# A two-block transformer kernel on one core: what TensorE computes over two waits ahead of the second feed forward

## The chip, the cores and the metric

The kernel is one program on one core of a Trainium2 chip. TensorE (PE in the profile) multiplies, with its weight loads shown apart as PEld. VectorE is DVE, ScalarE is ACT, GpSimd is POOL, and SyncE (SP) issues the transfers. The metric is the device time of one execution in microseconds. The kernel before took 2340.14 us, the median of three runs (2338.34, 2341.20 and 2340.14 us).

## The reference, cut to what matters

Two transformer blocks follow each other over 256 tokens of width 2048. The first mixes by a forgetting attention and a short convolution and has a SwiGLU feed forward. The second mixes by three branches and has a feed forward with a convolution. The place of the change lies between the second block's output projection and its feed forward:

```python
x = x + gt1 * (jnp.concatenate([o_mla, o_na, o_fn], axis=-1) @ w_out[l])
...
h2 = rmsnorm_2(x, g_ffn[l]) * (1 + sc2) + sh2
x = x + gt2 * conv_ffn(h2, w_up[l], conv_w[l], conv_b[l], w_down[l])
```

The root mean square norm of `x` takes a sum over all 2048 features of each token, and no part of `h2` is there before that sum.

## The kernel before, in words

All activations lie transposed in SBUF: features on the 128 partitions, the 256 tokens along the row, 16 tiles of 128 features. The weights are streamed from HBM once. Each chunk of 128x1024 values comes into one of four slots (`raw`), ACT rounds it to `hi` (line 586), DVE subtracts to get `lo` (line 1746), and TensorE makes three products for each tile of 128x128 weights (lines 1178 to 1180): `hi` by the rounded input, `hi` by the input's rest, `lo` by the rounded input. `hi`, `lo` and the inputs `hs`, `ysa`, `ysb` are of the type float32r, which TensorE takes in one pass. A product of operands of the type float32 ("plain" here) is made in two passes, so it leaves two records of matmul and two of weight load in the trace.

The order of the work is written out by hand, engine by engine. Engines meet in semaphores, and each engine runs its own list strictly in order. Around the change TensorE's list is:

1. the last products of the output projection `out2` (lines 1178 to 1180 on `ysa` and `ysb`);
2. `residual_stats("out2", "ffn2")`: plain products of one column (line 1247) that sum the squares of `x` over the partitions, two on `ssum` and four on `sqb`. ACT then takes the root (`std`, line 610), and DVE the reciprocal (line 1807);
3. a first `bridge`, whose products have no reader (line 1706);
4. `spread("ffn2", 5)`: it waits for the reciprocal and spreads it over the partitions with two plain products of 128 columns (line 1228);
5. a second `bridge`;
6. the first products of the feed forward, on `hs`. Before the three products of each of the first four feature tiles, TensorE waits for that tile: DVE multiplies `hg` by the spread row (line 2562), ACT rounds to the first half of `hs` (line 1118), and DVE makes the second half (line 2567).

The bridge's products go to bank 6 of PSUM, which nothing reads at that time. `ysb` is the rounded input of the projection that has just ended; its place is written next by the hidden layer of the feed forward, and `hg` and `hs` lie behind it.

Of the kernel before, what the change touches and what calls it, by code (L numbers as in the profile page):

```python
# [31 lines left out]
P = 128  # L32
D = 2048
KT = D // P
NX = 256
# [127 lines left out]
def build(nc, tokens, ctx_tokens, cols_d, tables1_d, tables2_d, stream, mod_stream, c_rows, na_bias_d, w_fnet_d, out):  # L163
    stack = ExitStack()
    with stack:
# [6 lines left out]
        start = -(-top[0] // 64) * 64  # L172
        top[0] = start

        def at(name, shape, dt, offset):
            size = 4 * int(np.prod(shape[1:]))
            assert offset + size <= limit, (name, offset + size, limit)
            return nc.alloc_sbuf_tensor_at(name, shape, dt, offset=offset)

        def keep(name, shape, dt=F32):  # L180
            offset = top[0]
            top[0] += -(-4 * int(np.prod(shape[1:])) // 64) * 64
            return at(name, shape, dt, offset), offset
# [9 lines left out]
        tabs, _ = keep("tabs", [P, N_TABS])  # L193
# [14 lines left out]
        ssum = at("ssum", [P, 2, NX], F32, o_rstd)  # L208
        mix_r = at("mix_r", [P, N1], F32, o_rstd)
        _, o_work = keep("work_slab", [P, 2, 4, N1])  # L210
        sq = at("sq", [P, 2, 4 * N1], F32, o_work)
        xn = at("xn", [P, 2, 4 * N1], F32, o_work)
# [45 lines left out]
        ysb = at("ysb", [P, 8, 2, NX], F32R, o)  # L258
# [26 lines left out]
        ps = stack.enter_context(nc.psum_tensor("ps", [P, 8, 512], F32))  # L285
# [7 lines left out]
        def tab(name):  # L293
            return tabs[:, TABS[name][0]:TABS[name][0] + TABS[name][1]]

        ident, mean = tab("ident"), tab("mean")
# [214 lines left out]
        def _(sp_):  # L511
# [29 lines left out]
            for ly in LAYERS:  # L541
                def body(it, ly=ly):
                    for hf in range(ly.halves):
                        for j in range(ly.c):
                            a = ahead(ly, it, hf, j)
                            if a is not None:
                                load(a[0], a[1])
                            for m, (where, _, _) in enumerate(ly.dots):
                                if where == hf * ly.c + j:
                                    load_mod(ly.mbase + m + it * len(ly.dots), m % 2)  # L550
                            if ly.name == "kv1" and (hf, j) == (0, 2):
                                sp_.dma_start(cols[:, KT:N_COLS], cols_d[:, KT:N_COLS]).then_inc(tables_in, 16)
                                sp_.dma_start(tabs[:, 0:N_TABS1], tables1_d).then_inc(tables_in, 16)
                            if ly.name == "kv1" and (hf, j) == (1, 2):
                                sp_.dma_start(cbx[:, :, :].rearrange("p a n -> p (a n)"), c_rows[0].partition_broadcast(P))\
                                   .then_inc(c_in, 16)
                            if ly.name == "up1a" and (hf, j) == (1, 0):
                                sp_.dma_start(cx[:, bass.ds(2 * it, 2), :], ctx_tokens[:, bass.ds(2 * it, 2), :]).then_inc(ctx_in, 16)
                            if ly.name == "dn1a" and (hf, j) == (0, 0):
                                sp_.dma_start(cx[:, bass.ds(it + 12, 1), :], ctx_tokens[:, bass.ds(it + 12, 1), :]).then_inc(ctx_in, 16)  # L560
                            if ly.name == "up1b" and (hf, j) == (0, 2):
                                sp_.dma_start(tabs[:, bass.ds(it * TAB_PIECE + TABS["swap"][0], TAB_PIECE)],
                                              tables2_d[:, bass.ds(it * TAB_PIECE, TAB_PIECE)]).then_inc(late_in, 16)
                            if ly.name == "conv1" and (hf, j) == (9, 0):
                                sp_.wait_ge(y_ready, HEADS)
                                sp_.dma_start(cbc[:, :, :].rearrange("p a n -> p (a n)"), c_rows[1].partition_broadcast(P))\
                                   .then_inc(c_in, 16)
# [582 lines left out]
        def _(pe):  # L1150
# [73 lines left out]
            def spread(name, bank, values=None):  # L1224

                pe.wait_ge(inv_ready, NTH[name] + 1)
                for th, rows in token_tiles(name):
                    ins = pe.matmul(ps[:, bank, th * P:th * P + rows], (tok_inv(name) if values is None else values)[0:rows, th:th + 1].to_broadcast([rows, P]),
                                    ident[0:rows, 0:rows], start=True, stop=True)
                ins.then_inc(rstd_ready, 1)  # L1230

            def residual_stats(name, norm, gain=False, before_last=None):
                halves = LY[name].its * LY[name].halves
                kinds = [(ssum, sqb, 0)] + ([(gsum, gsqb, 2)] if gain else [])
                tiles = 1 if name in FOLDED else 2
                last = tiles - 1 if name in ADDED else tiles + 1
                pe.wait_ge(sum_added, ADD0[name] + halves + 1 + (name in FOLDED) + 2 * (name in ADDED))
                pe.wait_ge(std_ready, NTH[norm])
                for i in range(last + 1):
                    if i >= tiles:  # L1240
                        pe.wait_ge(sum_sq, SUMS[name] + halves + i - tiles + 1)
                    if i == last and before_last is not None:
                        before_last()
                    for total, part, c0 in kinds:
                        x = total[:, i, :] if i < tiles else part[:, 1, i - tiles, :]
                        for th in range(2):
                            ins = pe.matmul(ps[:, 4 + c0 + th, 0:1], x[:, th * P:th * P + P], mean[:, 0:1],
                                            start=i == 0, stop=i == last)
                ins.then_inc(stat_ready, 1)
# [453 lines left out]

            def bridge(n):
                for _ in range(n):
                    pe.matmul(ps[:, 6, 0:NX], ident, tabs[:, 0:NX], start=True, stop=True)

            residual_stats("out2", "ffn2")
            bridge(2)
            spread("ffn2", 5)  # L1710
            bridge(4)
            for turn, (hf, j) in enumerate(KV_ORDER):
                if turn == 7:
                    opener(7, hs[:, 0])
# [28 lines left out]
        def _(dve):  # L1743
# [10 lines left out]
            def mod_dot(ly, it, m):  # L1754

                _, x_only, i = ly.dots[m]
                half = i % 2
                n = ly.mbase + m + it * len(ly.dots)
# [1011 lines left out]
```

## Time and profile before

| | us |
|---|---|
| median of three runs | 2340.14 |
| the profiled execution | 2339.23 |
| its span, first instruction to last | 2337.4 |
| PE busy in the span | 2327.6 |
| PEld busy | 2264.7 |
| DVE busy | 1662.2 |
| ACT busy | 1123.2 |

The profiled execution's own time is 1.8 us above its span, and 0.9 us below the median of the runs.

Three of the views need a word. In a timeline or a chain a row begins with its start and its duration in us, counted from the span's start; "x8" says that eight records in a row were merged, and the duration runs from the first one's start to the last one's end. Matmuls overlap, so the time from one start to the next is shorter than one record: for n merged records it is (duration minus one record) / (n - 1). In brackets stands the idle time ahead of a row, and what ended it. A row of "windows" gives the busy time and the count of each engine in a stretch, in the order PE, PEld, DVE, ACT, POOL, and then the granted share of TensorE's full clock (PEclk), the share of the DMA engines and GB/s. A row by line (L1725) gives the shortest, median and longest record in ns.

### The profile page before, as it was taken

The numbers are of one execution on the slowest core, as the hardware profiler recorded it, in microseconds if no ns is written. First come the engines' busy times: TensorE is split into PE (matmuls) and PEld (weight loads), VectorE is DVE, ScalarE is ACT, GpSimd is POOL, SyncE is SP. The second block draws the span as 40 slices with busy tenths as digits, with TensorE's granted clock in tenths as the row PEclk, the third lists the DMA queues.
The fourth block names the chain that finished last, engine by engine and source line by source line (L and its number), as shares of the span: only waits on it lengthen the run. The fifth ranks groups of instructions, "written<-read, shape, count | busy, mean of one in ns | idle before, by whom it ended". The sixth has DMA issues, their size and how long they took to land.

```text
span 2337.4 us, 49745 instructions
## 1 busy us (share of the span) xinstructions
PE 2327.6 (100%) x19268; PEld 2264.7 (97%) x19268; DVE 1662.2 (71%) x2504; ACT 1123.2 (48%) x1501; POOL 0.2 (0%) x4
## 2 busy tenths in 40 slices
PE   9999999999999999999999999999999999999998
PEld 9998899999999999999988989799999999999998
DVE  6676678788878887888887755467666566655665
ACT  6454446554445553445632342456554355544554
POOL 0000000000000000000000000000000000000000
PEclk9999999999999999999999999999999999999999
DMA  7875567588778887887567722054666656665664
GB/s 282 290 280 195 191 229 243 199 293 305 267 257 291 292 291 241 270 289 263 203 225 255 253 75 91 19 190 163 201 194 193 194 189 191 198 194 190 196 191 144
DMA packets 141889, 509.19 MB, mean 218 GB/s; under 512 B 15824, under 2 KB 17360, under 8 KB 141392
## 3 DMA queue, kind: packets, MB, share of 16 engines
q1 hardware_dynamic: 141776, 507.60, 64.9%
q8 instruction: 81, 1.33, 0.2%
q14 instruction: 32, 0.26, 0.0%
HBM read 505.44 MB, written 2.10 MB: 217 GB/s over the span
## 4 chain that ended last, share of the span: by engine, by line
PE 98%; DVE 1%; DMA 0%; ACT 0%; issue 0%; SPq 0%; ACTq 0%; DVEq 0%
PE ps L1178 30%; PE ps L1180 30%; PE ps L1179 30%; PE ps L1543 1%; PE ps L1561 1%; PE ps L1206 1%; PE ps L1207 1%; PE ps L1208 1%; PE ps L1364 1%; PE ps L1552 0%; PE ps L1346 0%; PE ps L1389 0%; PE ps L1370 0%; DMA raw<-in_stream 0%; PE ps L1609 0%; PE ps L1347 0%
## 5 line engine op out<-in xcount | busy, mean ns | idle before, releaser
L1746 DVE TENSOR_TENSOR lo<-raw,hi 128x1024 fp32r<-128x1024 f32 x751 | 915.7, 1222 | 477.5 <-ACT hi L586 473.9
L586 ACT ACTIVATE hi<-raw 128x1024 fp32r<-128x1024 f32 x753 | 797.1, 1061 | 950.6 <-PE ps L1180 843.5
L1178 PE MATMUL ps<-hs,hi 128*128 128x256 f32 (+1 forms) x3056 | 857.9, 281 | 0.4 <-DVE hs L2567 0.3
L1180 PE MATMUL ps<-hs,lo 128*128 128x256 f32 (+1 forms) x3056 | 857.2, 280 | 0.0
L1179 PE MATMUL ps<-hs,hi 128*128 128x256 f32 (+1 forms) x3056 | 857.2, 280 | 0.0
L1178 PEld LDWEIGHTS ps<-hs,hi 128*128 128x128 f32 x3056 | 573.6, 188 | 6.2 <-DVE hs L2567 0.8
L1179 PEld LDWEIGHTS ps<-hs,hi 128*128 128x128 f32 x3056 | 573.9, 188 | 5.2
L1180 PEld LDWEIGHTS ps<-hs,lo 128*128 128x128 f32 x3056 | 573.6, 188 | 5.1
L1178 PE MATMUL ps<-hid,hi 128*128 128x256 f32 x1408 | 388.6, 276 | 0.0
L1180 PE MATMUL ps<-hid,lo 128*128 128x256 f32 x1408 | 388.6, 276 | 0.0
L1179 PE MATMUL ps<-hid,hi 128*128 128x256 f32 x1408 | 388.6, 276 | 0.0
L1179 PEld LDWEIGHTS ps<-hid,hi 128*128 128x128 f32 x1408 | 264.3, 188 | 0.0
L1178 PEld LDWEIGHTS ps<-hid,hi 128*128 128x128 f32 x1408 | 264.3, 188 | 0.0
L1180 PEld LDWEIGHTS ps<-hid,lo 128*128 128x128 f32 x1408 | 264.3, 188 | 0.0
L1776 DVE SCALAR_TENSOR_TENSOR wm<-wm,cbx 128x1024 f32<-128x1024 f32 x192 | 233.7, 1219 | 4.9 <-DMA wm<-in_mod_stream 4.9
L1178 PE MATMUL ps<-xs,hi 128*128 128x258 f32 (+2 forms) x760 | 221.1, 291 | 0.4 <-DVE lo L1746 0.4
L1180 PE MATMUL ps<-xs,lo 128*128 128x258 f32 (+2 forms) x760 | 216.3, 285 | 0.0
L1179 PE MATMUL ps<-xs,hi 128*128 128x258 f32 (+2 forms) x760 | 215.8, 284 | 0.0
L1178 PEld LDWEIGHTS ps<-xs,hi 128*128 128x128 f32 x760 | 142.9, 188 | 4.6 <-issue 2.7
L1179 PEld LDWEIGHTS ps<-xs,hi 128*128 128x128 f32 x760 | 143.9, 189 | 0.0
L1180 PEld LDWEIGHTS ps<-xs,lo 128*128 128x128 f32 x760 | 142.9, 188 | 0.0
L600 ACT ACTIVATE cv<-ps,cols 128x256 f32<-128x256 f32 x88 | 44.9, 560 | 78.5 <-PE ps L1180 78.5
(335 smaller groups left out, 2537.8 us busy)
## 6 DMA issues: line engine op xcount, KB each, us to landing
raw<-in_stream SPq DMA_DIRECT2D x753, 512.0 KB, 4.3
wm<-in_mod_stream SPq DMA_DIRECT2D x192, 512.0 KB, 4.9
out_tokens<-y_final SPq DMA_DIRECT2D x4, 512.0 KB, 3.7
h<-in_tokens SPq DMA_DIRECT2D x3, 544.0 KB, 9.2
cx<-in_ctx_tokens SPq DMA_DIRECT2D x6, 256.0 KB, 5.9
cbx<-in_c_rows SPq DMA_DIRECT2D x1, 1024.0 KB, 7.5
cbc<-in_c_rows SPq DMA_DIRECT2D x1, 1024.0 KB, 7.9
na<-in_na_bias SPq DMA_DIRECT2D x1, 1024.0 KB, 4.7
```

Of the source, the lines that this page charges most:

```text
L586: act.activation(hi[:, slot, :], raw[:, slot, :], ACT.Copy).then_inc(hi_done, 1)
L600: act.activation(cv[:, t, hf, :], ps[:, 2 * hf + t, 0:NX], ACT.Identity, bias=dcol("conv2_b", it * 2 + c), scale=dcol("conv2_w1", it * 2 + ...
L1178: pe.matmul(acc_, hi[:, slot, w], x_hi, start=kt == 0, stop=False)
L1179: pe.matmul(acc_, hi[:, slot, w], x_lo, start=False, stop=False)
L1180: ins = pe.matmul(acc_, lo[:, slot, w], x_hi, start=False, stop=kt == last_k)
L1206: pe.matmul(acc_, x_hi, hi[:, slot, w], start=first, stop=False)
L1207: pe.matmul(acc_, x_lo, hi[:, slot, w], start=False, stop=False)
L1208: ins = pe.matmul(acc_, x_hi, lo[:, slot, w], start=False, stop=last)
L1364: ins = pe.matmul(ps[:, 7, NX:2 * NX], vtok[0:rows, kt, hd * P:hd * P + P], pt1[0:rows, kt, :], start=kt == 0, stop=kt == 2)
L1543: ins = pe.matmul(ps[:, score_bank2(hd, qt, local), :], q, k, start=i == 0, stop=i == len(terms) - 1)
L1746: dve.tensor_tensor(lo[:, slot, :], raw[:, slot, :], hi[:, slot, :].bitcast(F32), ALU.subtract)\
L1776: dve.scalar_tensor_tensor(w, w, 1.0, cbx[:, half, :], ALU.mult, ALU.mult, accum_out=mine[:, half:half + 1]).then_inc(wm_used, 1)
```

## The change

The products of `bridge` become another kind. Before, each was a plain one: the identity as weights, 256 columns of the table `tabs` as moving operand. Now each takes 128 columns of `ysb` as weights and 128 columns of another tile of `ysb` as moving operand, both float32r. Two become 14 ahead of the spread row, and four become 26 behind it. They go to the same bank, take no wait and signal nothing, as before.

```diff
             def bridge(n):
                 for _ in range(n):
-                    pe.matmul(ps[:, 6, 0:NX], ident, tabs[:, 0:NX], start=True, stop=True)
+                    pe.matmul(ps[:, 6, 0:P], ysb[:, 1, 0, 0:P], ysb[:, 2, 0, 0:P], start=True, stop=True)
 
             residual_stats("out2", "ffn2")
-            bridge(2)
+            bridge(14)
             spread("ffn2", 5)
-            bridge(4)
+            bridge(26)
```

On TensorE, from the last product of the output projection to the first of the feed forward, the list before is this; `ps` is PSUM, `std` the reciprocal row, a product is written output, inputs and shape, and xN counts products, not passes:

```order
 L1180 MATMUL ps<-ysa,lo 128x256
 L1247 MATMUL ps<-tabs,ssum 128x1 x2
 L1247 MATMUL ps<-tabs,sqb 128x1 x4
 L1706 MATMUL ps<-tabs 128x256 x2
 L1228 MATMUL ps<-tabs,std 128x128 x2
 L1706 MATMUL ps<-tabs 128x256 x4
 L1178 MATMUL ps<-hs,hi 128x256
```

The same stretch of TensorE's list in the changed kernel:

```order
 L1180 MATMUL ps<-ysa,lo 128x256
 L1247 MATMUL ps<-tabs,ssum 128x1 x2
 L1247 MATMUL ps<-tabs,sqb 128x1 x4
 L1706 MATMUL ps<-ysb 128x128 x14
 L1228 MATMUL ps<-tabs,std 128x128 x2
 L1706 MATMUL ps<-ysb 128x128 x26
 L1178 MATMUL ps<-hs,hi 128x256
```

Only the two groups of line 1706 differ; nothing moved past anything, and the lists of the other engines and of the transfers are the same.

## Rows read from the trace of the kernel before

**Rows 1.** The page: its first line, and the shares of the chain that ended last.
```profile
span 2337.4 us, 49745 instructions
PE 98%; DVE 1%; DMA 0%; ACT 0%; issue 0%; SPq 0%; ACTq 0%; DVEq 0%
```

**Rows 2.** The chain that ended last, 1603.9 to 1608.6 us, in order of time.
```profile
1603.90 0.97 PE ps L1706 x4
1604.88 0.46 PE ps L1228 x4
1605.36 0.43 DVE hg L2562
...
1608.61 0.39 PE ps L1178
```

**Rows 3.** Timeline of TensorE's matmuls (PE), 1603.8 to 1609.1 us.
```profile
1603.77 1.11 PE L1706 MATMUL ps<-tabs 128*128 128x256 f32 x4
1604.71 0.61 PE L1228 MATMUL ps<-tabs,std 128*128 128x128 f32 x4
1605.16 1.89 PE L1706 MATMUL ps<-tabs 128*128 128x256 f32 x8
1607.05 0.36 PE L1178 MATMUL ps<-hs,hi 128*128 128x256 f32 x1
...
1607.95 0.38 PE L1178 MATMUL ps<-hs,hi 128*128 128x256 f32 x1 [0.32 <-DVE hs L2567]
...
1609.07 0.33 PE L1178 MATMUL ps<-hs,hi 128*128 128x256 f32 x1
```

**Rows 4.** Timeline of TensorE's weight loads (PEld), 1602.8 to 1608.1 us.
```profile
1602.85 0.97 PEld L1247 LDWEIGHTS ps<-tabs,sqb 128*128 128x128 f32 x8 [0.32 <-ACT sqb L823]
1603.74 0.73 PEld L1706 LDWEIGHTS ps<-tabs 128*128 128x128 f32 x4
1604.50 0.63 PEld L1228 LDWEIGHTS ps<-tabs,std 128*128 128x128 f32 x4
1605.05 1.60 PEld L1706 LDWEIGHTS ps<-tabs 128*128 128x128 f32 x8
...
1607.95 0.19 PEld L1178 LDWEIGHTS ps<-hs,hi 128*128 128x128 f32 x1 [0.52 <-DVE hs L2567]
1608.06 0.19 PEld L1179 LDWEIGHTS ps<-hs,hi 128*128 128x128 f32 x1
```

**Rows 5.** Timeline of DVE: the reciprocal, and a tile of `hs`.
```profile
1604.23 0.17 DVE L1807 RECIPROCAL std<-std 128x2 f32<-128x2 f32 x1 [1.50 <-ACT std L610]
...
1607.41 0.48 DVE L2567 SCALAR_TENSOR_TENSOR hs<-hg,mod,hs 128x256 fp32r<-128x256 f32 x1
```

**Rows 6.** Weight loads by line: transposes of 16, of 128 columns, the bridge's.
```profile
L1357 PEld LDWEIGHTS ps<-tabs,p x16: 90/90/90, 167.2 to 283.6; 128*16 128x16 f32 x16
...
L1725 PEld LDWEIGHTS ps<-tabs,hg_final x32: 138/141/223, 2327.6 to 2331.4; 128*128 128x128 f32 x32
...
L1706 PEld LDWEIGHTS ps<-tabs x12: 190/190/192, 1603.7 to 1606.5; 128*128 128x128 f32 x12
```

**Rows 7.** The page: weight loads of float32r weights in the feed forwards.
```profile
L1178 PEld LDWEIGHTS ps<-hs,hi 128*128 128x128 f32 x3056 | 573.6, 188 | 6.2 <-DVE hs L2567 0.8
```

**Rows 8.** Windows: around the bridges, in the feed forward behind, and at the end.
```profile
1603.60:1607.00 3.40, 3.40 (x19) 2.79 (x18) 1.50 (x5) 2.46 (x5) 0.00 (x0) 1.00 0.20 81
1607.00:1610.40 3.40, 3.03 (x22) 2.62 (x22) 2.91 (x5) 1.18 (x3) 0.00 (x0) 1.00 0.00 0
...
1612.00:1640.00 28.00, 28.00 (x249) 27.95 (x248) 23.76 (x35) 18.96 (x28) 0.00 (x0) 1.00 0.53 174
...
2335.00:2337.40 2.40, 0.00 (x0) 0.00 (x0) 0.00 (x0) 0.00 (x0) 0.00 (x0) 0.62 0.65 242
```

**Rows 9.** Timeline of PE at the span's start.
```profile
1.50 5.49 PE L1275 MATMUL ps<-sq 128*128 128x256 f32 x12 [1.50 <-DVE sq L1847]
...
7.87 0.29 PE L1270 MATMUL ps<-xs,lo 128*128 128x272 f32 x1
```

**Rows 10.** Waits of PE, 1605 to 2320 us: in total, times, longest.
```profile
PE ps L1178 <- DVE hs L2567: 0.3, 1, 0.3
```

## Prediction

> **What bounds the kernel now.** I read the chain first: TensorE makes up 98% of it over 2337.4 us [rows 1], so a change on TensorE's list counts where it lies on that chain. Then the stretch of the change. The chain there runs through the first bridge, the spread row and DVE's `hg`, and comes back to TensorE at 1608.61, where it waits for a tile of `hs` [rows 2]. The second bridge is not in that list: it lies beside DVE's and ACT's work. So the first bridge can move the end, and the second only if it outlasts the tiles. Last, from 1605 us to 2320 the list of TensorE's waits has one entry, 0.3 us for `hs` [rows 10]. Behind this stretch nothing waits that could take up a delay: what is lost or won here stands in full at the end.
>
> **Is there a wait to be won?** The reciprocal ends at 1604.23 + 0.17 = 1604.40 [rows 5]. A tile of `hs` that DVE ends at 1607.41 + 0.48 = 1607.89 is followed by its weight load at 1607.95 [rows 4, 5], so waking takes 0.06, and the spread row's load could start at 1604.46. It starts at 1604.50, and its product, behind the bridge's last, at 1604.71 [rows 3, 4]. With nothing ahead, the product would start one load later than its load: 0.11, from 1607.95 to 1608.06 [rows 4]. That is 1604.57. The present bridge holds the chain up by 0.14 us, and this is the most that any other bridge can win.
>
> **The price of one new product.** No row of before shows a float32r product of 128 columns, so I bound it. Call the time from one to the next s.
> - By columns alone: in the feed forward 248 float32r products of 256 columns start in 28.00 us, 0.113 each [rows 8]. Half the columns give s = 0.057.
> - By weight loads: the eight one-column passes of line 1247 have next to nothing to stream, and still their loads stand (0.97 - 0.19) / 7 = 0.111 apart [rows 4]. The record of a float32r load lasts 188 ns and of a plain one 190 [rows 6, 7]; at 16 columns it is 90, so 128 columns cost 100 ns above a base that overlaps. A load of a transpose is 141, so other kinds exist, but float32r is not that kind. After a wait, with two loads free to run ahead, float32r loads too are 0.11 apart [rows 4]. This gives s = 0.111.
> - If under 256 columns the type were worked off as plain, in two passes with a load each: s = 2 x 0.111 = 0.222.
>
> I take 0.111, the nearest row in kind, since the weights of each product are loaded anew even though they are the same. 0.057 and 0.222 stay as the ends.
>
> The Trainium skill, TensorE: Matmul & The Clock Gate, section LDWEIGHTS, prices a load by its columns at 1.2 GHz, an estimate of 0.107 for 128, and the trace's 0.111 agrees. Its section Back-to-back issue gap instead gives some 81 ns per product for streams of load and product at 128 columns; by that 14 would cost 1.13 us and not 1.55. It speaks against my reading, and the one-column rows go against it here, so it stands as a rival.
>
> **The first bridge, 2 plain to 14.** Removed: two products, four passes of 256 columns, starting at 1603.77 [rows 3]. Added: 14 loads and products. The first load is at 1603.74 [rows 4]; the spread row's load follows 14 s later, at 1603.74 + 1.55 = 1605.29, and its product one load later, at 1605.40. Before it stood at 1604.71: later by 0.69. In general the delay is 14 s + 0.11 - 0.97, and at least -0.14. The waiting instruction behind it is the spread row itself, and behind that come `hg`, `hs` and all of the feed forward, which shift with it.
>
> **The second bridge, 4 plain to 26.** Before, it begins loading at 1605.05 and hides until the first tile's load, its product at 1607.05 [rows 3, 4]. That start has slack: the fourth tile's first product is at 1609.07 [rows 3], and ahead of it lie nine products, 9 x 0.113 = 1.02 us; if they start by 1608.05 in one piece, nothing is late. (The second tile is there by 1607.95, the third by 1608.61, both ahead of their turn then.) In the new kernel, on a clock shifted by the first bridge's delay, the 26 loads end at 1605.05 + 26 x 0.111 = 1607.94, and the first product starts at 1608.05. The cover is used up exactly and the cost is 0.0; at s = 0.113 it would be 0.05. If the cover were gone, each further ns of s costs 26 ns here and 14 in the first bridge.
>
> **The sum.** +0.69 + 0.0 to 0.05: about +0.7 us. Against the profiled execution: 2339.23 + 0.7 = 2339.9. The median of the runs was 0.91 above that execution, so 2340.9 us. DVE, ACT and the transfers have the same lists; they start 0.7 later in this stretch and wait as before. Bank 6 has no reader, and `ysb` is not rewritten until the hidden layer.
>
> **The clock.** PEclk is 1.00 in both windows of the stretch, the second of them with 0.37 us of idle time on PE [rows 8]. At its low level (1.2 GHz) the span begins: line 1275, two passes each, starts every (5.49 - 0.63) / 11 = 0.44 us, twice the 0.216 of line 1706 [rows 3, 9]. In the changed kernel the array streams 57 of each 111 ns in the bridges, where it now streams all the time, so less is streamed, though PE is never long without a product. The clock is lost in this trace only at the very end, PEclk 0.62 after the last product [rows 8]. I take it to hold.
>
> **Rivals.**
> 1. Columns alone decide, s = 0.057. Then the 14 are over at 1603.77 + 0.80 = 1604.57, just when the reciprocal lets the row go, so the full 0.14 is won; the 26 take 1.48 and end before `hs` is there. Time 2340.0. For it: two loads can overlap one product in the first of a burst. Against it: the one-column rows.
> 2. Loads overlap in part, s = 0.081: 1.13 + 0.11 - 0.97 = +0.27, the second bridge hidden, 2340.4. This is the page's figure above; the rows show no such spacing for full loads.
> 3. The slower side: the products are not one-pass ones on the chip, s = 0.222. First bridge: 3.11 + 0.11 - 0.97 = +2.25. Second: 5.77 from 1605.05 is 1610.82, its first product of the feed forward 1610.93 against 1608.05, +2.88. Together +5.1, 2345.3, slower by 0.22%. It decides from s = 0.211 on. For it: no float32r product under 256 columns is in the trace. Against it: on the changed list each is one entry, and those of 256 columns leave one record each [rows 3].
> 4. The clock falls in the stretch because half as much is streamed. At the start it took from 1.50 to about 7.6 us of products to rise (a record of 272 columns is back at 0.29 by 7.87) [rows 9]. 6.1 us at half speed cost 3.05, with the 0.7 makes +3.8, 2343.9. Should it fall in the first bridge and rise only after 6.1 us of dense work, the bridges run at twice 0.111 as in rival 3, and it is 5.1 + 3.05 = +8.2, 2348.3. Over 0.2% it comes if the low level lasts more than (4.7 - 0.7) x 2 = 8 us. The Trainium skill (same page, section Why this matters for your kernels) ties the loss to gaps without products; by that rule it would not fall here, and no row of before shows a stretch like the new one.
>
> **How the numbers follow.** Forecast (s of 0.108 to 0.125, +0.6 to +1.2) 0.65; rival 1 0.12; rival 2 0.07; rival 3 0.09; rival 4 0.05; something unseen 0.02. The runs of before lie 1.1 to 2.9 us apart, so medians of few runs move by about 1 us, more than most of these cases differ. About 0.2%, 4.7 us, is what a measurement of this kernel can tell from no change. Rivals 1 and 2 and the forecast lie inside; of rival 3 about half, with the runs' spread, lies above it, of rival 4 a third. Slower by over 0.2%: 0.07; faster: 0.01; within: 0.92. The range runs from 2338.8 (rival 1 less 1.2) to 2343.6 (the forecast's upper end, and rival 4's nearer case by the lower half of its spread).
>
> **What would show it.** In the profile after: 40 records on line 1706, one for each product, loads 0.111 apart, merged to about 1.6 and 3.0 us; the spread row's first product near 1605.4; DVE's first `hg` near 1606.05; no wait of PE for `hs` any more, or one under 0.1, and the fourth tile's first product near 1609.8; PEclk 1.00 throughout. Eighty records, or starts 0.06 or 0.08 apart, would make the price wrong; a spread row at 1604.6 is rival 1; a PEclk under 1.00 in this stretch is rival 4.

## The result, and the profile after

| | before | changed |
|---|---|---|
| median, us (13 runs each) | 2340.69 | 2345.47 |
| lowest to highest | 2338.34 to 2341.67 | 2340.27 to 2349.64 |
| ratio to before, 95% interval | | 1.0017 (1.0010 to 1.0024) |
| mean granted clock of a run | 1.000 in the profiled one | 1.000 in 5 runs, 0.996 to 0.998 in 8 |

The changed kernel is 4.8 us slower, and the spread of its runs tells more than the median: they fall into two groups. Five lie at 2340.3 to 2341.4 us, where the forecast of 2340.9 stood. Eight lie at 2343.9 to 2349.6 us, and these eight have the lower mean clock. The profile taken was one of the first group (2340.86 us, span 2338.6, clock 1.000), so at first it shows only the steps on the path, not the loss.

The changed kernel's matmuls, from the sums of squares to the tenth product on `hs` (start, duration, as in [rows 3]):

```profile
1603.37 1.05 PE L1247 MATMUL ps<-tabs,sqb 128*128 128x1 f32 x8 [0.24 <-ACT sqb L823]
1604.28 1.76 PE L1706 MATMUL ps<-ysb 128*128 128x128 f32 x14
1605.88 0.66 PE L1228 MATMUL ps<-tabs,std 128*128 128x128 f32 x4
1606.29 3.10 PE L1706 MATMUL ps<-ysb 128*128 128x128 f32 x26
1609.23 0.33 PE L1178 MATMUL ps<-hs,hi 128*128 128x256 f32 x1
...
1610.34 0.28 PE L1178 MATMUL ps<-hs,hi 128*128 128x256 f32 x1
```

Its weight loads in the two bridges, which answer to those of [rows 4]:

```profile
1604.26 1.64 PEld L1706 LDWEIGHTS ps<-ysb 128*128 128x128 f32 x14
...
1606.27 2.98 PEld L1706 LDWEIGHTS ps<-ysb 128*128 128x128 f32 x26
```

Forty records for forty products: they are one-pass ones. The loads start (2.98 - 0.19) / 25 = 0.112 us apart. Absolute times moved by 0.5 us ahead of the change already, so I count from the first product on `sqb`: 1603.37 here, 1602.85 before. The spread row's product comes 2.51 us behind it and came 1.86 behind it (+0.65). The first product on `hs` comes 5.86 behind it; the forecast's 1608.05, with 0.69 added, is 5.89. The tenth, the first of the fourth tile, comes 6.97 behind it and came 6.22 (+0.75): the nine products between take 1.11 us, not the forecast 1.02, and that is the last 0.1.

The chain of the changed kernel (compare [rows 2]):

```profile
1603.37 1.05 PE ps L1247 x8
1604.42 1.62 PE ps L1706 x14
1606.04 0.50 PE ps L1228 x4
1606.54 2.85 PE ps L1706 x26
1609.39 0.17 PE ps L1178
```

Where the chain ran through DVE and ACT, it now runs through the second bridge: the time in which that bridge was hidden behind their work is used up. A window over the stretch shows nothing amiss, and that is the trap:

```profile
1604.00:1608.00 4.00, 4.00 (x37) 4.00 (x37) 1.28 (x4) 2.58 (x6) 0.00 (x0) 1.00 0.20 79
```

PE is "busy" 4.00 of 4.00 us. But a record of a 128-column product lasts 275 ns, and its columns stream in about 57 (an estimate: half of the 0.113 us at which products of 256 columns start [rows 8]). With a product every 0.112 us the array streams about half of the time.

### The profile page after: what moved, and what is told of

The parts are those of the page before. It is cut to its first block, busy times and chain, and to the rows that moved or that the text cites. A ratio compares the mean times of both kernels' runs of the same rounds, so it can differ in the third digit from the quotient of the medians.

```text
span 2338.6 us, 49801 instructions
## 1 busy us (share of the span) xinstructions
PE 2328.6 (100%) x19296; PEld 2266.8 (97%) x19296; DVE 1662.0 (71%) x2504; ACT 1123.4 (48%) x1501; POOL 0.2 (0%) x4
## 4 chain that ended last, share of the span: by engine, by line
PE 98%; DVE 1%; DMA 0%; ACT 0%; issue 0%; SPq 0%; ACTq 0%; DVEq 0%
PE ps L1178 30%; PE ps L1180 30%; PE ps L1179 30%; PE ps L1543 1%; PE ps L1561 1%; PE ps L1206 1%; PE ps L1207 1%; PE ps L1208 1%; PE ps L1364 1%; PE ps L1552 0%; PE ps L1346 0%; PE ps L1389 0%; DMA raw<-in_stream 0%; PE ps L1370 0%; PE ps L1609 0%; PE ps L1347 0%
```

## The experiments

All were timed in 10 or 11 runs each, beside the kernel before on the same chip. Its median was 2340.05 us (33 runs) beside the changed kernel again, 256 columns, "7 and 15" and "none"; 2339.98 (33 runs) beside "first only", "second only" and the two plain ones; 2340.23 (20 runs) beside 192 and 64 columns. "Low clock" counts the runs with a mean granted clock of 0.998 or less. The path is read in each kernel's one profile as above, from the first product on `sqb` to the 10th and to the 100th on `hs`, against 6.22 and 16.49 us before (the changed kernel's first profile: +0.75 and +0.68). The last column is the stretch at the low level in that profile.

| kernel | median | ratio (95%) | low clock | 10th | 100th | low stretch |
|---|---|---|---|---|---|---|
| changed, again | 2345.70 | 1.0019 (1.0010 to 1.0028) | 8 of 11 | +5.41 | +5.52 | 10.2 us |
| 256 columns | 2342.14 | 1.0009 (1.0000 to 1.0018) | 0 of 11 | +1.06 | +1.39 | none |
| 192 columns | 2342.47 | 1.0006 (0.9997 to 1.0015) | 1 of 11 | +2.35 | +2.28 | 3.4 us |
| 64 columns | 2346.23 | 1.0023 (1.0014 to 1.0033) | 10 of 10 | +5.99 | +7.13 | 13.7 us |
| 7 and 15 | 2340.38 | 1.0003 (0.9994 to 1.0012) | 3 of 11 | -0.08 | -0.08 | none |
| none | 2341.42 | 1.0006 (0.9997 to 1.0015) | 9 of 11 | +0.19 | +1.57 | 6.8 us |
| first only | 2341.58 | 1.0007 (0.9998 to 1.0016) | 4 of 11 | +1.62 | +1.62 | 3.4 us |
| second only | 2339.47 | 0.9999 (0.9990 to 1.0008) | 1 of 11 | +0.05 | 0.00 | none |
| plain, 4 and 7 | 2341.14 | 1.0004 (0.9995 to 1.0013) | 0 of 11 | +1.01 | +0.94 | none |
| plain, 1 and 4 | 2339.66 | 0.9998 (0.9989 to 1.0007) | 0 of 11 | -0.15 | +0.23 | none |

Of the 86 runs of the kernel before that stand beside these, none is at 0.998 or less. The count has a limit: the profiles also show 0.3 to 3.7 us of the span's end at the low level, so a fall of 3.4 us shows as 0.998 or 0.999 and can be missed. "Low clock" counts the longer falls.

**The changed kernel again**, no edit.

> The changed kernel once more, 14 and 26 products of 128 columns. In 8 of its 13 runs the mean granted clock was 0.996 to 0.998 and the time 2343.9 to 2349.6 us; in the other 5 it was 1.000 and 2340.3 to 2341.4. Theory A (TensorE's array streams only half of the time in the stretch of the bridges, and its clock falls to the low level there in some executions): about half of the runs again at a mean clock under 0.999 and 3 to 8 us longer, and a profile of such a run shows PEclk under 1.00 from about the second bridge on, nowhere else. Theory B (the slow runs have a cause that is not in this stretch, such as transfers): the time is lost elsewhere, or spread over the span, and the share of slow runs does not follow the bridges.

(The change had 8, not 9, of its 13 runs at the low clock, where later expectations say 9 or 17 of 24: it is 16 of 24 with these.) Measured: 8 of 11 at the low clock, 2345.2 to 2347.2 us; the other three at 2340.1 to 2341.7. This time the profile is of an execution in which the clock fell. Its matmuls:

```profile
1603.28 1.05 PE L1247 MATMUL ps<-tabs,sqb 128*128 128x1 f32 x8 [0.24 <-ACT sqb L823]
1604.20 2.50 PE L1706 MATMUL ps<-ysb 128*128 128x128 f32 x14
1606.49 1.16 PE L1228 MATMUL ps<-tabs,std 128*128 128x128 f32 x4
1607.30 5.79 PE L1706 MATMUL ps<-ysb 128*128 128x128 f32 x26
1612.89 0.52 PE L1178 MATMUL ps<-hs,hi 128*128 128x256 f32 x1
1613.21 0.41 PE L1179 MATMUL ps<-hs,hi 128*128 128x256 f32 x1
```

and its windows (the column behind POOL is PEclk):

```profile
1602.00:1605.00 3.00, 2.68 (x23) 2.39 (x22) 1.34 (x5) 2.19 (x6) 0.00 (x0) 1.00 0.55 184
1605.00:1615.20 10.20, 10.20 (x50) 10.20 (x50) 6.45 (x13) 4.10 (x9) 0.00 (x0) 0.50 0.01 5
1615.30:1620.00 4.70, 4.70 (x44) 4.70 (x43) 1.65 (x2) 1.29 (x2) 0.00 (x0) 1.00 0.33 115
```

The clock falls to 0.50, that is 1.2 GHz, at 1605.0, in the middle of the first bridge, and comes back at 1615.3, some 2.4 us after the dense products on `hs` have begun. In between TensorE works at half the pace: the 26 products last 5.79 us and not 3.10, and those of 256 columns start 0.21 us apart and not 0.113. The tenth product on `hs` is 5.41 us late, the 100th 5.52. Apart from the span's two ends the clock is low nowhere else, so theory B falls for this run: the time is lost here.

**The same products with 256 columns.** Equal count and, by the loads, nearly equal time, but the array streams throughout.

```diff
-                    pe.matmul(ps[:, 6, 0:P], ysb[:, 1, 0, 0:P], ysb[:, 2, 0, 0:P], start=True, stop=True)
+                    pe.matmul(ps[:, 6, 0:NX], ysb[:, 1, 0, 0:P], ysb[:, 2, 0, 0:NX], start=True, stop=True)
```

> The same 14 and 26 one-pass products, but of 256 columns. By the weight loads (0.111 us) and the columns (0.113) they take nearly the same time, so the path is the same +0.7 to 0.8 us, but the array streams all of the time. Theory A: the clock is 1.000 in all runs, all within 2340 to 2343 us, median about 2341.5, ratio to before 1.0003. Theory B: slow runs as in the changed kernel, at a mean clock of 0.997 and 2344 to 2349 us. A third reading (it is the float32r products on ysb, or so many in a row, that lower the clock) also gives slow runs here.

Measured: no run at a low clock, as theory A has it. But the median is 2342.1 and not 2341.5, and the highest run 2344.4 and not 2343: in the profile the products of the second bridge started 0.12 us apart, not 0.113, and those of the feed forward behind them 0.118 (last section).

```profile
1605.50 3.36 PE L1706 MATMUL ps<-ysb 128*128 128x256 f32 x26
```

The two highest runs (2343.6 and 2344.4 us) are at 0.999; whether they hold a short fall is not shown. The reading that float32r products on `ysb` as such bring the long falls is out.

**192 columns** and **64 columns**, each with `ps[:, 6, 0:c]` and `ysb[:, 2, 0, 0:c]`, c = 192 or 64; the loads set the same pace.

> 14 and 26 one-pass products of 192 columns. The weight loads still set the pace (0.111 us; the columns would need 0.085), so the path is as in the changed kernel, +0.7 us, but the array streams three quarters of the time, not half. Theory A (the share of time in which the array streams decides, through the clock): the clock falls in clearly fewer runs than with 128 columns (17 of 24 so far), 0 to 3 of 11, median 2341 to 2342. Rival (any stream of float32r products bound by weight loads lowers the clock, whatever its columns): 7 or 8 of 11 at a mean clock of 0.996 to 0.998 and 2345 to 2347 us.

> 14 and 26 one-pass products of 64 columns, loads again 0.111 us apart: the path is +0.7 us or 0.05 less, and the array streams a quarter of the time. Theory A: the clock falls in nearly all runs (9 to 11 of 11) at a mean clock of 0.996 to 0.998, median 2345.5 to 2348. Rival: as with 128 columns, 7 or 8 of 11, median 2345.5.

Measured: 64 columns lose the clock in all 10 runs, 128 in 16 of 24, 192 clearly in one of 11 (its median of 2342.5 us is above the expected 2341 to 2342). But the profile of 192 shows a short fall in a run that counts as 0.999:

```profile
1605.60:1609.00 3.40, 3.40 (x18) 3.40 (x18) 2.08 (x5) 1.12 (x3) 0.00 (x0) 0.50 0.00 0
1609.00:1613.00 4.00, 4.00 (x37) 4.00 (x37) 3.24 (x7) 2.32 (x6) 0.00 (x0) 1.00 0.02 4
```

Five of its runs lie at 2339.2 to 2340.4 and six at 2342.5 to 2344.3 us, so falls of this length in about half of them are likely, though only the one is shown. With 64 columns the low level lasted longest, to 1618.0 us:

```profile
1602.00:1604.30 2.30, 1.98 (x17) 1.69 (x15) 1.12 (x3) 1.54 (x4) 0.00 (x0) 1.00 0.47 155
1604.40:1617.90 13.50, 13.50 (x65) 13.50 (x65) 8.36 (x15) 4.64 (x10) 0.00 (x0) 0.50 0.07 19
```

The number of products, of loads and their pace (0.112 us at the full clock, 0.213 at the low one) are one and the same with 64, 128 and 192 columns; only the columns differ, and with them how often the clock is low for long, and how long. The rival (any stream bound by loads) falls on 192 columns; between 64 and 128 the counts alone (10 of 10, 16 of 24) could still be chance.

One row of the kernel with 64 columns limits what may be said of the cause (line 1709 is the bridge's there):

```profile
1604.14 3.02 PE L1709 MATMUL ps<-ysb 128*128 128x64 f32 x14
```

The clock fell at 1604.32, 0.18 us behind the bridge's first product, when two of the 40 had started. In that execution the bridge can hardly have brought the fall; it can only have kept the clock low. What ran ahead of it, the sums' one-column products and the waits between them, stands in every kernel here, in the one before too.

**Shorter bridges of the new kind**: `bridge(7)` and `bridge(15)`.

> 7 and 15 products of 128 columns, so that both bridges last as long as before: 0.78 and 1.67 us against 0.86 and 1.72. On the path nothing is lost (0.0 to -0.1 us). Theory A: the array streams half of the time in as short a stretch as before; the clock falls in fewer runs than in the changed kernel, but in some; fast runs at 2340. If it is only the length of the bridges that matters (more time at half streaming), none is slow. Theory B: as many slow runs as in the changed kernel, or none, without relation.

Measured: the path is back (-0.08 us), and three of 11 runs, at 2341.5, 2344.0 and 2345.1 us and 0.997 or 0.998, still lose the clock. So half streaming loses it even in a stretch as short as before, but in fewer runs (3 of 11 against 16 of 24, which with so few runs makes it likely and not more). How long the stretch is seems to count as well.

**No bridge**: `bridge(0)` twice.

> No bridge products at all. The spread row's product starts when the reciprocal is there: 0.14 us won on the path, TensorE idle for some 0.6 us ahead of the spread row and 1.9 us ahead of the first tile of hs. Theory A: the array streams least of all, so the clock falls at least as often as in the changed kernel, and longer; fast runs 2340.0, slow ones 2344 or more. Theory B: no relation to streaming; time 2340.0 in all runs.

Measured: the clock is lower in nearly all runs, yet the median rises by 1.4 us only, and not one run is at the 2344 us or more that I expected of slow ones. The profile's windows:

```profile
1602.00:1606.00 4.00, 2.88 (x21) 2.32 (x19) 1.70 (x6) 2.77 (x6) 0.00 (x0) 1.00 0.45 158
1606.10:1612.80 6.70, 5.32 (x23) 5.14 (x24) 5.64 (x13) 3.52 (x8) 0.00 (x0) 0.50 0.00 0
```

Here the clock falls later (1606.1), lasts 6.8 us, and in part of it TensorE waits for `hs` anyway; the dense products begin 1.4 us into it and are not kept waiting by a bridge. I had reckoned with how often it falls and not with what stands in the low stretch. The experiment shows what the plain bridge is worth: 1.6 us at the 100th product in the one profile, 1.4 in the medians, where the interval of the ratio still includes none.

**One bridge of each kind**: 14 new products and 4 plain; then 2 plain and 26 new. Of the first kernel's edit one place is shown; the lines by which `bridge` chooses the kind are left out.

```diff
-            bridge(26)
+            bridge(4, plain=True)
```

> Only the first bridge changed: 14 products of 128 columns, then 4 plain ones. The path: the first bridge's +0.7 us and nothing in the second. Theory A (the clock falls because the array streams only about half of the time over the whole stretch from the sums to hs): the half streaming ends with the spread row, after some 3.5 us, then 1.7 us of full streaming follow; the clock falls in fewer runs than the 9 of 13 and 8 of 11 of the full change, 0 to 3 of 11, median 2340.8, slow ones 2345 to 2347. Rival (the first bridge alone brings the fall): as many slow runs as in the full change.

> Only the second bridge changed: 2 plain products, then 26 of 128 columns. The path: the 26 products just fill the time until the tiles of hs are there, +0.0 to 0.1 us. Theory A: 2.9 us of half streaming behind 0.9 us of full streaming; the clock falls in some runs, fewer than with both (2 to 6 of 11), median 2340.1, slow ones 2343 to 2346. Rival (the second bridge alone brings the fall): 7 or 8 of 11 at a mean clock of 0.997.

Measured for the first alone: 4 of 11 clearly low and not 0 to 3, 2341.6 us and not 2340.8, no run at 2345 or more, and a short fall in the profile:

```profile
1604.50:1607.80 3.30, 3.30 (x15) 3.03 (x14) 0.87 (x3) 0.95 (x3) 0.00 (x0) 0.51 0.04 15
1608.00:1612.00 4.00, 3.95 (x29) 3.60 (x28) 3.24 (x7) 1.57 (x5) 0.00 (x0) 1.00 0.00 0
```

The clock falls at 1604.5, as in the changed kernel in the first bridge, but comes back at 1607.9 behind the plain products: 3.4 us low and not 10.2, 0.9 us lost on the path beside the 0.75 of the new bridge. For the second alone: one of 11 low (2343.9 us) where 2 to 6 were expected, median that of before within the noise, the path +0.05. So neither does alone what both do. That the second new bridge keeps low a clock that has fallen ahead of it fits one profile of each kernel. That the first one makes it fall is not shown (see 64 columns).

**Plain products for as long as the new ones**: 4 and 7.

> Bridges as long as the changed kernel's, but of plain products of 256 columns as before: 4 (1.72 us) and 7 (3.0 us). The array streams all of the time. The path: 4 x 0.43 - 0.86 = +0.86 us for the first, 0.0 to 0.1 for the second. Theory A: the clock is held in all 11 runs, median 2341.0, highest under 2343. Rival (it is the length of the bridges that brings the fall, whatever runs in them): slow runs of 2344 and more at a clock of 0.997.

Measured: no run at a low clock, 2341.14 us. The length of the bridges alone does not bring the long falls. Two runs are at 2343.3 and 2343.4 us, above what was expected, at a clock of 0.999. The kernel before has runs like them: beside these, three of its 33 are at 2342.2 to 2343.0 us, at 0.999 too. The cause is open.

**One plain product ahead of the spread row, four behind it.**

> One plain product ahead of the spread row, not two, and 4 behind it, all as before. The bridge's last pass then ends before the reciprocal is there. The path: 0.14 us won, 2340.0 against 2340.1, which the runs cannot tell from none. Theory A: TensorE idles some 0.2 us more, the clock is held: 2340.0. A rival (the clock is so near its edge in this stretch that the shorter bridge loses it in some runs): one or more of 11 at 0.998 and 2342 or more.

Measured: the path 0.15 us shorter, no run at a low clock, ratio 0.9998 (0.9989 to 1.0007). It is no slower, and not measurably faster. No kernel here beats the one before.

## Why the prediction was wrong

- **The price of one new product, 0.111 us, by its weight load**: right, 0.112. Neither the 0.057 of the columns, nor the 0.081 of rival 2, nor the 0.222 of two passes. Rivals 1 to 3 fall: forty records, and no such spacing.
- **The first bridge, +0.69**: +0.65. **The second, hidden to the last, 0.0 to 0.05**: hidden it was, and both together are +0.75; the 0.1 beyond the first bridge comes from the nine products on `hs`, which I had put at 0.113 us each. **The sum of 0.7**: where the clock holds, the runs have a median of 2341.0 us (8 of the 24), the forecast 2340.9. That they agree to 0.1 us is luck: these eight runs spread over 1.6 us, and the median of before was 2340.69 us in one set of runs and 2340.05 in the other, not 2340.14.
- **The clock, "I take it to hold"**: this is the step that failed, a term put at nothing. The clock falls in two runs of three, and that makes the median. The fall had a chance of 0.05 as rival 4. The condition that rival 4 names, that half as much is streamed, is borne out by the runs with 192 and 256 columns. Its two cases, +3.8 and +8.2 us, lie on both sides of what was measured: 16 runs with a median of 2346.1 (+5.4 against the 2340.69 of before), with 10.2 us at the low level in the one profiled. In that run the loss is below the upper case because the clock fell 0.8 us into the first bridge and because 2.4 us of dense products, and not the 6.1 us of the span's start, went by before it rose. The chance is what was far off.
- **Why the chance was off.** I had computed that the array would stream 57 of each 111 ns, and set against it that PEclk was 1.00 in both windows of the stretch [rows 8] and that PE is never long without a product. But in those windows the plain bridge streamed all the time, and the change takes just that away. The rows of before could not speak for a stretch that none of them has, and "I take it to hold" had nothing else to rest on.
- **The rule on gaps.** The Trainium skill (TensorE: Matmul & The Clock Gate, section Why this matters for your kernels) ties the loss to gaps without products. The trace disagrees: in the changed kernel's second profile the clock fell with a load every 0.112 us, in a bridge without a gap, and the longest idle time of PE from 1602 us to the fall was 0.24 us. By the Trainium skill, same page, section The HAM clock gate, the clock goes by how busy TensorE has been. The busy time of the profile is not the measure of it here: in their bridges PE is 100% busy with 64 columns as with 192, and the clock is clearly low in 10 of 10 runs and in one of 11.

What is shown: the fall in this stretch, its size, and that long falls come more often with 128 columns than with 192 or 256 at an equal or nearly equal pace. What is likely: that the length of the stretch counts. What stays open: why the one execution loses the clock and the next does not. Nothing in the kernel differs between them. It was not tried whether the sums' one-column products ahead of the bridge tip it, nor whether the kernel before has short falls in its longer runs; the one profile of it shows none.

## What to carry to other kernels

Reckon filler for TensorE in columns streamed over time, not in products or in busy time. A product of 64 to 192 columns with its own weight load was bound by the load here (0.112 us), and the profile shows TensorE busy all the while. Where a filler keeps up a clock, ask of each other filler what share of the time it streams. Put a price on the lost clock before giving it a chance: up to half the low stretch, 4.7 us on the path for 10.2 us low here, and less where TensorE waits anyway, 1.6 for 6.8 without a bridge. And where runs fall into two groups, look at the clock of each run before reading the one profile.

## What the runs showed that was not expected

- The low level stayed for 3.4, 3.4, 6.8, 10.2 and 13.7 us in the five profiles with a fall, and the dense products behind did not bring it back at once: 2.4 us in the changed kernel, 4.6 with 64 columns. At the low level the loads of 128 columns start 0.213 us apart, nearly twice 0.112, so load-bound products too go at about half the pace.
- Products of the feed forward can start 0.118 us apart in place of 0.113 at the full clock. Before, 91 matmuls stand in the window from 1611 to 1621 us:

```profile
1611.00:1621.00 10.00, 10.00 (x91) 10.00 (x90) 9.31 (x15) 7.21 (x15) 0.00 (x0) 1.00 0.32 107
```

With one plain product ahead and four behind there are 88, at the same clock:

```profile
1611.00:1621.00 10.00, 10.00 (x88) 10.00 (x87) 8.94 (x13) 7.05 (x14) 0.00 (x0) 1.00 0.28 86
```

It costs that execution 0.7 us from the tenth to the 200th product on `hs`, more than the 0.15 won ahead of it, and it is why the kernel with 256 columns ended 1.7 us late and not 1.1. Within some 20 us the spacing was 0.113 again. What sets it is open.
